# Two transformer blocks in float32: transitions of the second block as a pipeline of tiles

## The chip, the cores and the metric

The kernel runs on one core of a Trainium2 chip. The metric is the device time of one execution, in microseconds (us). Engines: PE multiplies matrices (PEld is its weight load), DVE and ACT work on vectors, POOL is the general engine, SP issues transfers.

## What is computed

A first block (latent and dilated attention, then a convolutional FFN) and a second, modulated block (attention, Fourier and Hyena mixers, then an FFN) run two layers each over 256 tokens of width 1024. The second block carries 256 context tokens through its layer 0; in layer 1 only keys and values are taken from them. Everything is float32. The parts that matter here are the second block's norms, shifts and gates:

```python
def rmsnorm_2(x, g):
    xf = x.astype(jnp.float32)
    y = xf * lax.rsqrt(jnp.mean(xf * xf, axis=-1, keepdims=True) + NORM_EPS)
    return (y * g.astype(jnp.float32)).astype(x.dtype)
...
        hx = rmsnorm_2(x, g_pre_mix[i]) * (1.0 + sc1) + sh1
        hc = rmsnorm_2(ctx, g_pre_mix[i]) * (1.0 + csc1) + csh1
        px = hx @ w_in[i]
...
        x = x + ga1 * rmsnorm_2(mix_x, g_post_mix[i])
...
        fx = rmsnorm_2(x, g_pre_ffn[i]) * (1.0 + sc2) + sh2
        yx = conv_ffn_2(fx, w_up[i], w_ffn_conv[i], b_ffn_conv[i], w_down[i])
        x = x + ga2 * rmsnorm_2(yx, g_post_ffn[i])
```

`sh`, `sc` and `ga` are slices of silu(c) @ w_mod + b_mod, one set for x and one for the context.

## The kernel before

**Matmuls.** A float32 product is made of three matmuls on high and low halves (`mm3`, L579, all recorded at L556). Features lie transposed in `hH`, `hL` (recorded as `hHL`). Weights come from HBM through `ring`, four slots of 1 MB, issued by SP in a fixed order (L1015). A piece of up to 1024 columns is copied to its high half by ACT (L1761, `wH`) and its low half subtracted by DVE (L1186, `wL`), by `splits_to` on both; three pieces rotate (`PIECES`), and `piece_used` gives one back. `piece_order` (L657) gives the last three pieces of a projection bank by bank. PSUM's eight banks are in two sets of four, `psv` read by DVE and `pss` read by ACT, opened in turn by `open_`, which waits for the bank's last reader.

**Order.** The program of each engine is written by hand. Each engine runs its instructions in that order, and semaphores join them (`V_full`, `S_free`, `root_ready` and so on), so an instruction that waits holds up all behind it on its engine.

**Stages.** First block, twice: features, `in` projections, latents (squares of the latent rows on ACT, small steps on DVE), lifts, rotary and dilated heads, attention, `out`, features, `up` with a convolution, `down` (22 pieces). Its own transitions already work by halves: add a half from PSUM to x (L1233, L1239), square the halves, `normalise1` with the gain as a broadcast row (L1249), transposes on PE (L606), high half by ACT and low half by DVE from PSUM (L1259). The next stage starts row by row (`have_rows`).

Second block, twice: modulation (`modulation_row` multiplies silu(c) by a chunk of w_mod, `modulation_col` turns it into columns `modc`; chunks `start`, `pairs`, `ffn`, `end` stand at different places), features, `hy`, q, k, v, Fourier, attention, `out`, features, `up`, `down`. Its transitions: ACT's `branch` copies odd tiles from PSUM to `mixo` and squares whole rows (`sumsq`, L1785 to L1788), DVE copies the even ones; `post` on DVE scales `mixo` by the inverse root and the gate row `gg` (L1594) and adds to x (L1596). Then `sumsq` of x, and `to_features`: four small steps of `inverse` (L1167 to L1173), a scaling by the row's inverse root (L1204), transposes, a scaling by gain column and shift column from PSUM (DVE L1216, ACT L1758) into `raw_h`, the high half by ACT and the low half by DVE (L1224). `have_features` lets the next stage begin when every tile is split. `modulation_ready` holds ACT's squares until the modulation columns exist. `keep_clock` issues matmuls without use, which fill PE's waits. POOL casts the FFN's products (L1038), and at the end stores x (L1054).

## Time and profile before

| | us |
|---|---|
| median of 3 runs | 1771.72 |
| lowest, highest | 1769.87, 1773.66 |
| profiled execution, its own time | 1769.04 |
| its span | 1767.3 |
| PE busy | 1639.4 (93%) |
| DVE busy | 1124.4 (64%) |
| ACT busy | 848.6 (48%) |
| POOL busy | 262.0 (15%) |

The span is the stretch from the first to the last recorded instruction; the execution's own time lies 1.7 us above it. The shares are averages over stages, so they say which engine bounds most of the time and not what a wait costs. The page's slices put PE's granted clock at nine tenths of full speed or more almost everywhere, with short dips.

### The profile page before, as it was taken

Reading aid. Unit: us, or ns where it says so; the run is one execution under the profiler, and the core shown is the slowest. Engines: PE = TensorE matmul, PEld = TensorE weight load, DVE = VectorE, ACT = ScalarE, POOL = GpSimd, SP = SyncE. Lnnn points to the kernel's source line nnn. Section 1 sums busy time; section 2 is a strip of 40 time slices with the busy share of each in tenths; the row PEclk is TensorE's granted clock in tenths of the full one; section 3 lists DMA queues with packets and bytes.
Section 4 is the critical chain, followed back from the end, with each engine's and each line's share of the span. In section 5 each row is a group of like instructions: output and inputs, shape, how many; then the busy total and the mean of one; then the engine's idle time right before and its main releaser. Section 6 shows DMA issues by size and latency. Waiting matters only on the chain. (4 is left out here: it accounts for less than half of the span.)

```text
span 1767.3 us, 22843 instructions
## 1 busy us (share of the span) xinstructions
PE 1639.4 (93%) x8628; PEld 1317.5 (75%) x8628; DVE 1124.4 (64%) x1875; ACT 848.6 (48%) x1518; POOL 262.0 (15%) x322
## 2 busy tenths in 40 slices
PE   7989999999999999899899899999999797989996
PEld 7667887886677887678467588888787595668875
DVE  5686898465868995553673744444333756579964
ACT  5554776355556664431353533333212534566742
POOL 2000113600021117000000001111630000001171
PEclk9999999999999999999999899999999799989998
DMA  7465765554578555523273533333222342246651
GB/s 261 151 209 172 202 189 180 193 167 166 198 225 246 145 170 169 161 78 96 94 237 111 155 96 96 96 96 96 96 95 96 102 138 66 72 124 187 184 185 48
DMA packets 266495, 258.32 MB, mean 146 GB/s; under 512 B 8821, under 2 KB 208729, under 8 KB 266130
## 3 DMA queue, kind: packets, MB, share of 16 engines
q1 hardware_dynamic: 262706, 245.36, 45.7%
q0 software_dynamic: 3536, 11.42, 1.8%
q8 instruction: 70, 1.15, 0.3%
q14 instruction: 39, 0.32, 0.1%
q10 hardware_dynamic: 144, 0.07, 0.0%
HBM read 255.72 MB, written 1.10 MB: 145 GB/s over the span
## 5 line engine op out<-in xcount | busy, mean ns | idle before, releaser
L556 PE MATMUL psv<-hHL,wH 128*128 128x512 f32 (+1 forms) x1952 | 644.2, 392 | 25.0 <-issue 21.1
L1186 DVE TENSOR_TENSOR wL<-ring,wH 128x1024 fp32r<-128x1024 f32 (+2 forms) x364 | 450.5, 1243 | 269.8 <-ACT wH L1761 266.7
L1761 ACT ACTIVATE wH<-ring 128x1024 fp32r<-128x1024 f32 (+2 forms) x364 | 376.1, 1040 | 302.1 <-PE psv L556 295.6
L556 PE MATMUL psv<-hHL,wL 128*128 128x256 f32 (+1 forms) x1504 | 468.5, 311 | 0.0
L556 PEld LDWEIGHTS psv<-hHL,wH 128*128 128x128 f32 x1952 | 368.2, 191 | 108.6 <-issue 23.3
L556 PE MATMUL psv<-wH,hHL 128*128 128x512 f32 (+2 forms) x936 | 319.2, 390 | 30.4 <-DVE wL L1186 17.6
L556 PEld LDWEIGHTS psv<-hHL,wL 128*128 128x128 f32 x1504 | 287.3, 191 | 15.9
L556 PE MATMUL pss<-wH,hHL 128*128 128x512 f32 (+3 forms) x808 | 274.4, 385 | 0.0
L556 PEld LDWEIGHTS psv<-wH,hHL 128*128 128x128 f32 x936 | 175.7, 189 | 74.4 <-DVE wL L1186 24.9
L556 PE MATMUL psv<-wL,hHL 128*128 128x512 f32 (+2 forms) x468 | 180.1, 385 | 0.0
L556 PEld LDWEIGHTS pss<-wH,hHL 128*128 128x128 f32 x808 | 152.5, 190 | 29.4
L1028 POOL TENSOR_TENSOR W<-scr 128x256 f32<-128x256 f32 (+1 forms) x88 | 81.7, 929 | 568.9 <-ACT scr L1918 568.9
L556 PE MATMUL pss<-wL,hHL 128*128 128x512 f32 (+3 forms) x404 | 155.2, 384 | 0.0
L1313 DVE SCALAR_TENSOR_TENSOR scr<-psv,colp,scr 128x510 f32<-128x510 f32 x44 | 33.0, 749 | 125.7 <-ACT scr L1910 125.7
L1761 ACT ACTIVATE scr<-psv 128x256 f32<-128x256 f32 x132 | 50.6, 384 | 126.7 <-PE psv L556 126.7
L1910 ACT ACTIVATE scr<-psv,colp 128x512 f32<-128x512 f32 x44 | 34.4, 781 | 155.0 <-PE psv L556 155.0
L556 PEld LDWEIGHTS psv<-wL,hHL 128*128 128x128 f32 x468 | 88.3, 189 | 16.1 <-issue 0.2
L1040 POOL TENSOR_TENSOR hHL<-W,hHL 128x256 fp32r<-128x256 f32 (+1 forms) x88 | 95.3, 1082 | 7.0
L556 PEld LDWEIGHTS pss<-wL,hHL 128*128 128x128 f32 x404 | 76.8, 190 | 14.6
L1314 DVE SCALAR_TENSOR_TENSOR scr<-scr,colp 128x255 f32<-128x255 f32 x132 | 79.7, 603 | 4.7
L1882 ACT ACTIVATE scr<-scr,colp 128x256 f32<-128x256 f32 x132 | 78.2, 592 | 2.3 <-DVE scr L1412 2.3
L1313 DVE SCALAR_TENSOR_TENSOR scr<-scr,colp 128x255 f32<-128x255 f32 x132 | 69.5, 526 | 4.3
(239 smaller groups left out, 1702.3 us busy)
## 6 DMA issues: line engine op xcount, KB each, us to landing
ring<-in_w_up SPq DMA_DIRECT2D x176, 512.0 KB, 5.2
ring<-in_w_mod SPq DMA_DIRECT2D x96, 512.0 KB, 4.8
ring<-in_w_down SPq DMA_DIRECT2D x88, 512.0 KB, 4.3
ring<-in_w_in SPq DMA_DIRECT2D x52, 512.0 KB, 4.6
ring<-in_w_out SPq DMA_DIRECT2D x32, 512.0 KB, 4.7
ring<-in_w_in SPq DMA_DIRECT2D x8, 384.0 KB, 6.0
ring<-in_w_in SPq DMA_DIRECT2D x8, 288.0 KB, 6.9
ring<-in_w_ukv SPq DMA_DIRECT2D x4, 512.0 KB, 4.2
```

Of the source, the lines that this page charges most:

```text
L556: return pe.matmul(o, a, b, start=start, stop=stop, skip_group_check=True)
L1028: gp.tensor_tensor(act[:, j, 0:ntok], cbuf(2 * j)[:, 0:ntok], cbuf(2 * j + 1)[:, 0:ntok], ALU.mult).then_inc(ffn_act, mark("ffn_act", ph, j))
L1040: gp.tensor_tensor(lo, a, hi.bitcast(F32), ALU.subtract).then_inc(act_split, mark("act_split", ph, j))
L1186: v.tensor_tensor(lo, raw, hi.bitcast(F32), ALU.subtract).then_inc(piece_split, told("piece_split", p))
L1313: return v.scalar_tensor_tensor(cv[:, :, 1:SEQ], bv_[:, :, 0:SEQ - 1], w0, cv[:, :, 1:SEQ], ALU.mult, ALU.add)
L1314: return v.scalar_tensor_tensor(cv[:, :, 0:SEQ - 1], bv_[:, :, 1:SEQ], w2, cv[:, :, 0:SEQ - 1], ALU.mult, ALU.add)
L1761: return ac.activation(o, i, ACT.Copy)
L1882: ac.activation(cbuf(n)[:, 0:SEQ], cbuf(n)[:, SEQ:2 * SEQ], ACT.Identity, scale=col(wname, l * 132 + 44 + u), bias=col(bname, l * 44 + u)) ...
L1910: ac.activation(cbuf(2 * j + g)[:, 0:ntok], b[:, 0:ntok], ACT.Identity, scale=col(wname, l * 132 + 44 + u), bias=col(bname, l * 44 + u)).t ...
```

## The change

In the second block, norm gains become rows: the columns (1 + scale) x gain are transposed by PE (`mix_rows`, `gates`), stored to DRAM and loaded back by POOL as `gain_rows`, broadcast to all partitions, for the mixer of the first layer in the middle of block 1's last FFN, for that of the second in the middle of layer 0's FFN. The normalise is one operation with the gain row (`normalise2`). The shift is added by PE: a matmul of `shift_rows` (its high and low halves) with `pick`, a selection matrix, into the bank of the transposes. The high and low halves are read from PSUM (`high_features2`, `low_features2`), and `raw_h` is gone; `xn4` holds four tiles of normalised rows. The post-norm works by halves: ACT squares each half in PSUM (`post_half`), DVE multiplies it by the gate row from PSUM (`gate_half`), and one operation scales and adds to x (`residual`). `transition` puts tiles behind one another on DVE and on ACT. The next stage begins at the last tile's first rows. The modulation at a layer's end moves into that transition. The context tiles of layer 0 are normalised and transposed inside block 1's last `down` (`CONTEXT_AT`).

In all four `down` projections the last piece's turn comes after two banks (`late`). In block 1 the small steps are three (`inverse1`), the dilated heads' transposes and copies come before the last input projection, the squares of the latents are taken together, and the first two pieces of `out` are split inside the attention's tail and no longer before it. x is stored from SP (tile 0, half of tile 1) and ACT (the other half), no longer from POOL.

```diff
-        raw_h = w_at(T0 + 4096, 2, KD, P)
+        gain_rows = w_at(T0 + 4096, 2, D)
+        xn4 = w_at(T0 + 6144, 4, D)
...
+        CONTEXT_AT = {11: 2, 13: 3}
...
+            def feature_tile(ph, t, x, banks=None):
+                pe.wait_ge(rows_normalised, at("rows_normalised", ph, t))
+                for (kind, b), k0 in zip(banks or feature_banks(ph, t), (0, 4)):
+                    for k in range(4):
+                        settle(pe.matmul(b[:, k * P:(k + 1) * P], x[:, (k0 + k) * P:(k0 + k + 1) * P], ident[:, :], start=k == 0, stop=False,
+                                         is_transpose=True, skip_group_check=True))
+                    c = 16 + 8 * (t // 2) + k0
+                    mm(b.rearrange("p (k n) -> p k n", k=4), shift_rows[:, :], pick[:, c:c + 4].unsqueeze(2).to_broadcast([64, 4, P]),
+                       False, True).then_inc(FULL[kind], mark(kind + "_full", ph, "hT", t))
...
+                turns = [(i, q) for i in range(len(banks)) for q in range(m, n)]
+                if late:
+                    turns = [(i, q) for i in (0, 1) for q in range(m, n - 1)] + [(0, n - 1), (1, n - 1)] + turns[2 * (n - m):]
...
-                for (t, h, kind, b), j, w in piece_order(banks, NJ, True):
+                for (t, h, kind, b), j, w in piece_order(banks, NJ, True, True):
                     if (t, h) == (0, 0):
+                        if ahead and j in CONTEXT_AT:
+                            c = CONTEXT_AT[j]
+                            feature_tile(context, c, xn[:, c % 2, :], ahead[c])
...
+            sp.wait_ge(residual_updated, at("residual_updated", ("b2", L - 1), "ffn", 0, 1))
+            sp.dma_start(out[0, 0:P, :], xs[:, 0, :]).then_inc(out_stored, mark("out_stored", "all", by=16))
+            sp.wait_ge(residual_updated, at("residual_updated", ("b2", L - 1), "ffn", 1, 1))
+            sp.dma_start(out[0, P:2 * P, 512:D], xs[:, 1, 512:D]).then_inc(out_stored, mark("out_stored", "all", by=16))
+            sp.wait_ge(out_stored, at("out_stored", "all"))
+            sp.wait_ge(half_stored, 16)
...
+            def load_mix_rows(l):
+                gp.wait_ge(gate_stored, at("gate_stored", l, "mix"))
+                load(gain_rows[:, :, :], rows_of(mix_dram[l], 2), "gain_rows_in", l, "mix")
...
-                        v.tensor_scalar(xn[:, t % 2, :], xs[:, t, :], rr[:, t:t + 1], None, ALU.mult).then_inc(rows_normalised, told("rows_normalised", ph, t))
...
+            def gate_half(ph, what, stage_, t, h):
+                kind, key, n = "VS"[t % 2], (ph, what, h, t) if what == "out" else (ph, what, t, h), slice(h * 512, (h + 1) * 512)
+                v.wait_ge(gate_in, at("gate_in", ph, stage_))
+                v.wait_ge(sum_of_squares, at("sum_of_squares", ph, "post", stage_, t, *(() if h else ("half",))))
+                v.tensor_tensor(mixo[:, t, n], bank(kind, *key), gg[:, t // 2, n], ALU.mult).then_inc(FREE[kind], told(kind + "_free", *key))
...
+            def residual(ph, what, stage_, t):
+                kind, key = "VS"[t % 2], (ph, what, 1, t) if what == "out" else (ph, what, t, 1)
+                v.wait_ge(root_ready, at("root_ready", ph, "post", stage_, t))
+                inverse1(4 + t)
+                v.wait_ge(FREE[kind], at(kind + "_free", *key))
+                v.scalar_tensor_tensor(xs[:, t, :], mixo[:, t, :], rr[:, 4 + t:5 + t], xs[:, t, :], ALU.mult, ALU.add).then_inc(residual_updated, told("residual_updated", ph, stage_, t))
...
+            def normalise2(ph, t, x):
+                v.wait_ge(root_ready, at("root_ready", ph, t))
+                inverse1(t)
+                v.wait_ge(gain_rows_in, at("gain_rows_in", ph[1], ph[2]))
+                v.scalar_tensor_tensor(x, xs[:, t, :], rr[:, t:t + 1], gain_rows[:, t // 2, :], ALU.mult, ALU.mult).then_inc(rows_normalised, told("rows_normalised", ph, t))
...
+            def transition(ph, what, stage_, nph, first, cs):
+                nt = 4 if ph[1] == 0 else 2
+                for t in range(nt):
+                    if t >= 2:
+                        normalise2(nph, t - 2, xn4[:, t - 2, :])
+                    for h in range(1 if what == "out" else 0, 2):
+                        gate_half(ph, what, stage_, t, h)
+                    residual(ph, what, stage_, t)
+                normalise2(nph, nt - 2, xn4[:, nt - 2, :])
+                splits_to(first, 0)
+                normalise2(nph, nt - 1, xn4[:, nt - 1, :])
+                for c in cs[:-1]:
+                    modulation_col(1, c)
+                for t in range(nt):
+                    low_features2(nph, t, cs)
+                    if t == 1:
+                        for c in cs[-1:]:
+                            modulation_col(1, c)
...
-                splits_to(first_piece[ph, "out", 0], 1)
...
+                attention(ph, units1, 0, MOD1[l]["pairs"], mla_columns, (first_piece[ph, "out", 0], (8, 9)))
...
+                if l == L - 1:
+                    nph = ("b2", 0, "mix")
+                    splits_to(first_piece[ph, "down"] + 8, 0)
+                    v.wait_ge(block2_in, at("block2_in", "all"))
+                    v.wait_ge(ffn_act, at("ffn_act", ph, NJ - 1))
+                    for t in (2, 3):
+                        normalise2(nph, t, xn[:, t % 2, :])
+                        splits_to(first_piece[ph, "down"] + 2 * t + 5, 0)
+                    for t in (2, 3):
+                        splits_to(first_piece[ph, "down"] + 2 * t + 8, 0)
+                        low_features2(nph, t)
...
+            def post_half(ph, what, stage_, t, h):
+                kind, bk, key = "VS"[t % 2], (ph, what, h, t) if what == "out" else (ph, what, t, h), (ph, "post", stage_, t)
+                ac.wait_ge(FULL[kind], at(kind + "_full", *bk))
+                if h:
+                    other_half(bank(kind, *bk), 4 + t, t, *key)
+                else:
+                    half_sum(bank(kind, *bk), t, *key)
...
+            def transition(ph, what, stage_, nph, first, cs):
+                nt = 4 if ph[1] == 0 else 2
+                last_key = (ph, what, 1, nt - 1) if what == "out" else (ph, what, nt - 1, 1)
+                def norm(t):
+                    ac.wait_ge(residual_updated, at("residual_updated", ph, stage_, t))
+                    sumsq(xs[:, t, :], D, t, nph, t)
+                def row(i):
+                    if i >= len(cs):
+                        return
+                    ac.wait_ge(S_free, at("S_free", *last_key))
+                    ac.wait_ge(S_full, at("S_full", "modrow", 1, cs[i]))
+                    if i:
+                        ac.wait_ge(V_full, at("V_full", "modcol", 1, cs[i - 1]))
+                    copy(mrow[:, :], bank("S", "modrow", 1, cs[i])).then_inc(S_free, mark("S_free", "modrow", 1, cs[i]))
+                for t in range(nt):
+                    for h in range(1 if what == "out" else 0, 2):
+                        post_half(ph, what, stage_, t, h)
+                    if nt == 4 and t in (1, 2):
+                        norm(t - 1)
+                if nt == 2:
+                    norm(0)
+                    splits_to(first, 0)
+                    norm(1)
+                else:
+                    norm(2)
+                    row(0)
+                    splits_to(first, 0)
+                    norm(3)
+                    row(1)
+                for t in range(nt):
+                    high_features2(nph, t)
...
+                attention(ph, units1, mla_columns, (first_piece[ph, "out", 0], (8,)))
...
+            ac.wait_ge(residual_updated, at("residual_updated", ("b2", L - 1), "ffn", 1, 0))
+            ac.dma_start(out[0, P:2 * P, 0:512], xs[:, 1, 0:512]).then_inc(half_stored, 16)
```

On DVE, in the second block's layer 0, from its output projection to its FFN (T2 below). `xs` is x (four tiles of 128 tokens, the last two of context), `W` here the mixed rows, gains or normalised rows, `rr` the inverse root. Before, from the update of tile 2 on:

```order
L1596 TENSOR_TENSOR xs<-xs,W 128x1024
L1167 RECIPROCAL rr<-root 128x1
L1169 TENSOR_TENSOR nwt<-rr 128x1
L1171 SCALAR_TENSOR_TENSOR nwt<-nwt,ss 128x1
L1173 SCALAR_TENSOR_TENSOR rr<-nwt,rr 128x1
L1594 SCALAR_TENSOR_TENSOR W<-W,rr 128x1024
L1596 TENSOR_TENSOR xs<-xs,W 128x1024
L1167 RECIPROCAL rr<-root 128x1
L1169 TENSOR_TENSOR nwt<-rr 128x1
L1171 SCALAR_TENSOR_TENSOR nwt<-nwt,ss 128x1
L1173 SCALAR_TENSOR_TENSOR rr<-nwt,rr 128x1
L1204 TENSOR_SCALAR scr<-xs,rr 128x1024
```

Now, from the update of tile 1 on:

```order
L1304 SCALAR_TENSOR_TENSOR xs<-W,rr,xs 128x1024
L1346 RECIPROCAL rr<-root 128x1
L1348 SCALAR_TENSOR_TENSOR nwt<-rr,ss 128x1
L1350 SCALAR_TENSOR_TENSOR rr<-nwt,rr 128x1
L1311 SCALAR_TENSOR_TENSOR W<-xs,rr,W 128x1024
L1296 TENSOR_TENSOR W<-psv,W 128x512
L1346 RECIPROCAL rr<-root 128x1
L1348 SCALAR_TENSOR_TENSOR nwt<-rr,ss 128x1
L1350 SCALAR_TENSOR_TENSOR rr<-nwt,rr 128x1
L1304 SCALAR_TENSOR_TENSOR xs<-W,rr,xs 128x1024
L1346 RECIPROCAL rr<-root 128x1
L1348 SCALAR_TENSOR_TENSOR nwt<-rr,ss 128x1
```

The first normalise (L1204 before, L1311 now) stood behind all four updates; it now stands behind tile 1's, and the gates (L1296) read PSUM.

On DVE a little further on, the end of that same hand-over. Before, the last tiles' features and then the weight halves of the FFN's first pieces (L1186):

```order
L1204 TENSOR_SCALAR scr<-xs,rr 128x1024
L1341 TENSOR_TENSOR modc<-psv,colp 128x2x4
L1216 TENSOR_SCALAR W<-psv,modg,modc 128x128 x4
L1224 TENSOR_TENSOR hHL<-W,hHL 128x8x128
L1216 TENSOR_SCALAR W<-psv,modg,modc 128x128 x4
L1224 TENSOR_TENSOR hHL<-W,hHL 128x8x128 x2
L1186 TENSOR_TENSOR wL<-ring,wH 128x1024 x3
L1313 SCALAR_TENSOR_TENSOR scr<-psv,colp,scr 128x2x255
```

Now, from the third tile's normalise on:

```order
L1311 SCALAR_TENSOR_TENSOR W<-xs,rr,W 128x1024
L1252 TENSOR_TENSOR wL<-ring,wH 128x1024
L1346 RECIPROCAL rr<-root 128x1
L1348 SCALAR_TENSOR_TENSOR nwt<-rr,ss 128x1
L1350 SCALAR_TENSOR_TENSOR rr<-nwt,rr 128x1
L1311 SCALAR_TENSOR_TENSOR W<-xs,rr,W 128x1024
L1468 TENSOR_TENSOR modc<-psv,colp 128x2x4
L1320 TENSOR_TENSOR hHL<-psv,hHL 128x4x128
L1320 TENSOR_TENSOR hHL<-pss,hHL 128x4x128
L1320 TENSOR_TENSOR hHL<-psv,hHL 128x4x128
L1320 TENSOR_TENSOR hHL<-pss,hHL 128x4x128
```

One weight half (L1252) now stands ahead of the last tile's normalise, and the low halves (L1320) are taken straight from PSUM.

On ACT, in the first block's layer 0, around the attention's end; `wH<-ring` is the high half of a weight piece, `scr,den<-pss,mx` the exponentials. Before:

```order
L1761 ACTIVATE scr<-pss 128x512 x2
L1864 ACTIVATE scr,den<-pss,mx 128x256 x4
L1761 ACTIVATE scr<-pss 128x512 x2
L1864 ACTIVATE scr,den<-pss,mx 128x256 x4
L1761 ACTIVATE scr<-pss 128x512 x4
L1810 ACT_TABLE_LOAD
L1810 ACTIVATE root<-eps_col 128x1
L1761 ACTIVATE wH<-ring 128x1024 x6
```

Now:

```order
L2049 ACTIVATE scr,den<-pss,mx 128x256 x4
L1898 ACTIVATE scr<-pss 128x512 x2
L2049 ACTIVATE scr,den<-pss,mx 128x256 x4
L1898 ACTIVATE scr<-pss 128x512 x2
L1898 ACTIVATE wH<-ring 128x1024
L1898 ACTIVATE scr<-pss 128x512 x2
L2007 ACT_TABLE_LOAD
L2007 ACTIVATE root<-eps_col 128x1
L1898 ACTIVATE wH<-ring 128x1024 x7
```

One weight copy now stands among the attention's last copies; before, the output projection's first pieces were split ahead of the attention.

## Rows read from the trace of the kernel before

**Rows 1.** The page, part 1: busy time of each engine, share of the span, instructions.
```profile
PE 1639.4 (93%) x8628; PEld 1317.5 (75%) x8628; DVE 1124.4 (64%) x1875; ACT 848.6 (48%) x1518; POOL 262.0 (15%) x322
```

**Rows 2.** Table by stretch: length, PE, PEld, DVE, ACT, POOL busy, PE's granted clock, DMA, GB/s.
```profile
733.15:755.43 22.28, 14.11 (x75) 10.31 (x73) 18.29 (x50) 18.70 (x39) 0.00 (x0) 0.80 0.31 95
755.43:760.50 5.07, 5.07 (x12) 4.01 (x13) 2.16 (x2) 0.34 (x1) 0.00 (x0) 0.51 0.57 180
982.55:1009.24 26.69, 17.93 (x110) 11.50 (x109) 24.09 (x58) 21.36 (x46) 0.53 (x1) 0.88 0.71 197
...
1377.04:1410.33 33.29, 20.54 (x105) 14.86 (x103) 24.86 (x63) 22.06 (x49) 0.00 (x0) 0.77 0.47 127
...
1543.93:1560.70 16.77, 8.78 (x40) 7.03 (x39) 14.27 (x30) 12.86 (x26) 0.53 (x1) 0.85 0.10 32
...
1752.23:1767.30 15.07, 0.39 (x2) 0.00 (x0) 5.26 (x8) 2.23 (x5) 1.13 (x2) 0.66 0.18 70
165.68:172.69 7.01, 6.34 (x54) 4.41 (x53) 6.52 (x12) 4.75 (x11) 0.54 (x1) 1.00 0.52 146
```

**Rows 3.** Timeline of PE: start, us, engine, line, operation, [idle before <-releaser].
```profile
755.43 1.19 PE L556 MATMUL psv<-hHL,wH 128*128 128x512 f32 x2 [5.58 <-issue]
...
1385.33 1.86 PE L556 MATMUL psv<-fold,mrow 128*128 128x2 f32 x8 [4.33 <-DVE mrow L1335]
```

**Rows 4.** Timeline: five rows of T1, and two of block 1's own transition.
```profile
736.51 0.16 DVE L1167 RECIPROCAL rr<-root 128x1 f32<-128x1 f32 x1 [1.80 <-ACT ss L1788]
...
737.29 0.75 DVE L1204 TENSOR_SCALAR scr<-xs,rr 128x1024 f32<-128x1024 f32 x1
...
738.10 0.66 PE L606 MATMUL pss<-ident,scr 128*128 128x128 f32 x4 [1.21 <-DVE scr L1204]
...
740.04 1.36 DVE L1216 TENSOR_SCALAR W<-psv,modg,modc 128x128 f32<-128x128 f32 x4
...
752.96 1.23 DVE L1224 TENSOR_TENSOR hHL<-W,hHL 128x1024 fp32r<-128x1024 f32 x1 [0.18 <-ACT hHL L1761]
...
169.16 1.28 DVE L1249 SCALAR_TENSOR_TENSOR scr<-xs,rr,W 128x1024 f32<-128x1024 f32 x1
...
170.37 0.68 DVE L1259 TENSOR_TENSOR hHL<-psv,hHL 128x512 fp32r<-128x512 f32 x1
```

**Rows 5.** Timeline of SP in T2, and the page's part 6: KB each, median us to landing.
```profile
984.81 14.48 SPq L1015 DMA_DIRECT2D ring<-in_w_up  x8
...
ring<-in_w_up SPq DMA_DIRECT2D x176, 512.0 KB, 5.2
```

**Rows 6.** Timeline of POOL in block 1's last FFN, and part 6 for a row broadcast.
```profile
684.58 1.40 POOL L1038 CAST hHL<-W 128x256 fp32r<-128x256 f32 x1
...
W<-gate_scratch POOLq DMA_DIRECT2D x2, 1024.0 KB, 6.0
```

**Rows 7.** Groups of PE by line with their idle time, and two waits in the timeline.
```profile
L556 PE MATMUL psv<-wH,hHL 128*128 128x512 f32 (+2 forms) x936 | 319.2, 390 | 30.4 <-DVE wL L1186 17.6 <-POOL hHL L1040 4.8 <-DVE scr L1314 3.6
...
L556 PE MATMUL psv<-W 64*128 64x256 f32 (+5 forms) x114 | 23.9, 417 | 9.4 <-DVE W L1543 8.6 <-DVE modc L1341 0.8
...
353.92 0.50 PE L556 MATMUL psv<-wH,hHL 128*128 128x512 f32 x1 [1.28 <-DVE wL L1186]
...
41.36 0.50 PE L556 MATMUL psv<-wH,hHL 128*128 128x512 f32 x1 [2.61 <-DVE wL L1186]
```

**Rows 8.** Timeline at the end of block 1's first attention, ACT and PE.
```profile
141.62 1.28 ACT L1810 ACT_TABLE_LOAD   x1
...
143.73 0.50 PE L556 MATMUL psv<-wH,hHL 128*128 128x512 f32 x1 [0.98 <-DVE hHL L1193]
144.07 0.40 PE L556 MATMUL psv<-wL,hHL 128*128 128x512 f32 x1
144.30 0.40 PE L556 MATMUL psv<-wH,hHL 128*128 128x512 f32 x1
```

**Rows 9.** Timeline of POOL at the end.
```profile
1758.65 1.13 POOL L1054 DMA_DIRECT2D out<-xs  x2 [27.78 <-DVE xs L1596]
```

484 lines of the change are left out of this document (264 added, 220 removed).

## The prediction

> **What bounds the kernel now.** I read the busy shares first: the matmul engine PE works 1639.4 of 1767.3 us, 93% of the span, DVE 64%, ACT 48% [rows 1]. So only the places where PE idles, or is kept busy with filler, can give time back. Next the timeline of PE, and the table by stretch, over each place where one stage hands to the next. Five stretches stand out [rows 2]: from the last matmul of block 1 to the first of block 2 (22.28 us, call it T1), block 2 layer 0 from its output projection to its FFN (T2, 26.69), its FFN to layer 1's mix (T3, 33.29), layer 1's output projection to its FFN (T4, 16.77), and the end (T5, 15.07). PE's busy time inside them (14 of 22 us in T1) is mostly filler, transposes and modulation. The same table has block 1's own transition, which already works by halves from PSUM with the norm gain as a row: 7.01 us, at a granted clock of 1.00. After T1 the granted clock stands at 0.51 for 5.07 us [rows 2], the 1.2 GHz level, PE having waited 5.58 us just before [rows 3]. The rest of PE's idle time is in short waits on the weight halves and on the attention's inputs [rows 7, 8].
>
> **T1.** Today the first features come by a chain: squares of all of x, four small DVE steps (736.51 to 737.29, 0.78 us), the scaling 0.75, transposes, gain and shift per column 1.36, the low halves from SBUF 1.23 for each of four tiles [rows 4]. The new chain is that of block 1: three small steps and a row-form normalise of 1.28, transposes, low halves from PSUM at 0.68 per 512 columns [rows 4]. I take block 1's 7.01 us, and add 0.9 for four 512-column shift matmuls on PE and the wait for both latent tiles: 7.9, so -14.4. The context tiles' transposes move into block 1's last down projection, where PE is the bound: four transposes take 0.66 [rows 4], so 16 take 2.6 at most, less where they cover a wait; with four shift matmuls and none of it hidden I charge +2.7. At 7 us of hand-over block 1 keeps its clock, so half of the 5.07 slow us goes too: -2.5. T1 in all -14.2 (bounds -9 to -17: the clock stays slow; the transposes hide).
>
> One new wait is on the way there. The context tiles' normalise on DVE waits for the gain rows, which POOL loads after its eighth FFN cast and subtraction, some 2.4 us behind the cast at 684.58; a 1024 KB broadcast takes 6.0 us to land [rows 6], so they are there at 693, and the normalise is through at 694.3. Queued behind it on DVE is a weight half that PE needs at 696.0. It is hidden by 0.5 to 1.5 us; a load of 9 us would cost 2 to 3, once.
>
> **T2.** Before, four residual updates, each a scaling and an addition of 1024 columns (1.28 and 1.23 by their like in [rows 4]), come before the first normalise. After, tile 0 is normalised as soon as tile 1's residual is in. Let E be the last matmul. The four output banks end 4.1 us apart (three pieces of six matmuls, one each 0.23 us [rows 8]). On DVE a residual or a normalise costs 1.28 plus three small steps of 0.2, 1.88 us; a gate of half a tile from PSUM about 0.7, like the low half's 0.68. Walking the queue: tile 0 normalised before E, tile 2's residual E+0.2, tile 1 normalised +2.1, tile 3's gate and residual +4.7, tile 2 normalised +6.6. Then, ahead of tile 3's normalise, DVE splits the first weight piece. Its DMA is issued after the modulation chunk frees the slot, at E+2 (984.81), and lands 5.2 later [rows 5], ACT copies it by E+8.2, DVE is through at 9.4, tile 3 normalised at 11.8 (ACT's part of the small steps included), and eight low halves at 0.61 to 0.68 end at 16.8. The FFN takes all four tiles as one moving operand, so it starts at E+17: -9.7. Without the wait for the weight it would be 14, -12.7; if gates wait for their squares too, 20, -7.
>
> **T3.** The same queue, plus two modulation columns that must come before the features. Before, they stood behind the whole post-norm chain (PE waits 4.33 us for them at 1385.33 [rows 3]) and the features began only after them. After, they follow the last normalise, and modulation's last rows are made a layer ahead. The same walk gives 17.5 of 33.29: -15.8 (bounds -12 to -19).
>
> **T4.** Two tiles. Tile 1's last gate at E+1.8, residual 3.9, squares and normalise 8.6, transposes, high and low halves of the second tile to 11.0 of 16.8: -5.5 (bounds -4 to -7). I give T2 to T4 no clock back: they stay over 10 us with filler inside.
>
> **T5.** Before, whole-row squares follow the last copy, then scaling and addition, and only then POOL issues both stores at 1758.65, 1.13 us of issuing [rows 9], some 6 us behind the last matmul (1752.2 [rows 2]). After, one square of 512 is left behind the last matmul, a gate of 0.7, three small steps, and two 512-column updates of 0.7; tile 0 is stored 3 to 4 us earlier and tile 1 in two quarter-megabyte stores from two queues. x is ready 3.6 instead of 5.9 us after the last matmul (-2.3). From the issue to the span's end is now 8.65 us (1767.3 less 1758.65); without POOL's 1.13 of serial issuing, and with half the bytes left behind the last update, I take 6.85: -1.8. Together -4.1 (bounds -1 to -6). The Trainium skill, "DMA: Bandwidth & Descriptors" (Issuing engine by pattern, and Latency), says that DMAs issued from SyncE or ScalarE have their first byte after about 0.6 us against 1 us from GpSimd, and that most of a DMA's fixed part of some 2 us is the write receipt, which halving the bytes doesn't touch. By that page alone the store would give 0.4 plus the smaller transfer; no row here shows the two issuers at the same store.
>
> **Short waits.** In each of four down projections PE waits 1.28 us for DVE's half of the last piece (the first at 353.92 [rows 7]; the others are alike). Taking that piece's turn after two banks gives DVE 2 us more: 4 x 1.28 = -5.1. The latents' squares are now taken in a batch with four small operations after them, and a third piece is split ahead of them. PE's wait of 2.61 there in layer 0, with about half as much in layer 1, goes but for 0.4: -3.5; all waits of this form for DVE's weight halves are 17.6 us [rows 7], so this and the tails make half of them. Attention start: the dilated transposes and copies go ahead of the last input bands, and DVE no longer splits the output's first pieces there. PE's waits there, 8.6 us in the two layers [rows 7], go: with 0.6 of a shorter queue before it -4.7 in layer 0, and -6.0 in layer 1, where a wait for a weight half before the bands shrinks too. The two splits come back inside the attention's tail. There DVE's second split follows ACT's copy, which stands behind the 1.28 us table load at 141.62; it pushes the last cast of the attention's output by 2.5 us and the projection that starts at 143.73 [rows 8] to 146.3: +2.6, and +1.5 in layer 1, where modulation covers more. Net -2.1 and -4.5. Small: -0.5 for shorter inverses in block 1, +1.5 for the row transposes, shift splits and their places in queues.
>
> **Sum.** -14.2 -9.7 -15.8 -5.5 -4.1 -5.1 -3.5 -6.6 +1.0 = -63.5. Against the profiled run's own 1769.04 that is 1705.5; the median of the runs is 2.7 above that run, so 1708.2.
>
> **A rule against the change.** The old normalise, one tensor times a per-row scalar from SBUF, takes 0.75 us for 1024 columns, the new one with a gain tensor 1.28 [rows 4]. The Trainium skill, "VectorE: DVE Perf Modes" (Mode 2x_2P, and Rules for kernel authors), says the first form gets twice the rate in float32 by using both read ports, a form with two tensors doesn't, and anything from PSUM doesn't either; it advises a copy to SBUF where many operations follow. The trace agrees (753 against 1284 ns). For 14 tiles the price is 14 x 0.53 = 7.4 us of DVE, of which the part on the path is in my walks. If that part outweighed the rest, T1 to T4 would lose 7.4 of their 45 us and the time be 1716. But each tile sheds 1.36 + 1.23 - 2 x 0.68 = 1.2 us of DVE, and ACT's 1.5 of scaling, so I give it no case of its own.
>
> **Rivals.** (a) The first weight piece isn't late, or its split doesn't hold up the last normalise: T2 and T3 at 14 us, 6 less: 1702. For it: block 1's first weights are there in a 7 us hand-over. Against: the slot is freed by the same modulation chunk. 0.2. (b) New waits eat a third of T1 to T4: gates must wait for ACT's squares of the same bank and hold banks that the transposes want, and the clock stays at 1.2 GHz after T1. T1 12, T2 21, T3 23, T4 13.5: +16, and +2.5 of clock; 1727. For it: ACT and DVE are in one chain per tile, and the walk has each hand-over at its shortest. 0.27. (c) The attention's splits cost more than the waits they replace (the change doesn't do there what it says): instead of -6.6, +4, other things as forecast: 1719. 0.1. (d) Slower: the clock. T1 shows a half-rate stretch after a wait. If the new order, with less filler in front of each stage, left PE at 1.2 GHz for long stretches, each us of full-speed work there costs one more; it decides once 64 us of such work run at half clock beyond what does so now, and 68 give 1776. The stretch seen after T1 is 5.07 us, so it has 0.03.
>
> **How the numbers follow.** Forecast 0.4 (1703 to 1715), (a) 0.2, (b) 0.27, (c) 0.1, (d) 0.03. The predicted time is the likeliest, 1708. The range leaves out (d), the lower edge of (a) and the worst of (b): 1695 to 1731. About 0.2% (3.5 us) is what a measurement of this kernel can tell from no change; all cases but (d) are faster by more: 0.96 faster, 0.01 the same, 0.03 slower.
>
> **What would show it.** In the profile after: PE from last to first matmul 8, 17, 17.5 and 11 us at T1 to T4; a granted clock of 1.00 behind T1; DVE's first weight split at T2 waiting for ACT with the last normalise behind it; no 1.28 us waits late in the down projections; attention starting within 1 us of PE's last work, its projection some 2 us later than its last cast would allow; two half stores and no POOL at the end. Wrong would be: a T2 over 20 us with the gates waiting for ACT, a DVE wait for the gain rows around 693 with PE idle behind it, or a clock below 0.9 over a whole stage.

## The result, and the profile after

The changed kernel takes 1717.4 us (median; runs from 1712.1 to 1719.4) against 1770.8 before: a ratio of 0.970, interval 0.968 to 0.972. The profiled run took 1718.0 and spans 1716.2. So 51.1 us of span went, where 63.5 were forecast. (Of the kernels under Experiments, one execution took 4138 us and another 9223, for no reason that the record shows; neither enters a number.)

The page of the changed kernel, its first line, the busy times that answer to [rows 1], and the group of PE that answers to the first of [rows 7]:

```profile
span 1716.2 us, 22859 instructions
...
PE 1642.1 (96%) x8638; PEld 1314.7 (77%) x8638; DVE 1108.8 (65%) x1816; ACT 833.4 (49%) x1520; POOL 265.6 (15%) x329
...
L564 PE MATMUL psv<-wH,hHL 128*128 128x512 f32 (+2 forms) x936 | 321.5, 393 | 22.6 <-DVE wL L1252 7.5
```

PE works as long as before (1642.1 us against 1639.4); what went is idle time. In this group the waits for a weight half fell from 17.6 to 7.5 us.

The table by stretch of the changed kernel: T1, the stretch behind it, T2, T3, T4, T5, then block 1's first output projection. Columns are those of [rows 2]:

```profile
730.93:740.28 9.35, 8.77 (x55) 5.19 (x53) 7.81 (x13) 7.21 (x14) 0.00 (x0) 1.00 0.64 196
740.28:745.35 5.07, 5.07 (x24) 4.18 (x23) 1.51 (x2) 0.06 (x1) 0.00 (x0) 1.00 0.76 262
965.20:987.42 22.22, 19.77 (x106) 12.65 (x105) 13.43 (x27) 10.64 (x24) 1.59 (x3) 0.85 0.89 240
1352.25:1375.35 23.10, 20.44 (x106) 12.76 (x105) 14.58 (x30) 10.94 (x26) 0.00 (x0) 0.85 0.68 182
1505.91:1521.70 15.79, 13.50 (x51) 9.57 (x49) 11.57 (x20) 9.43 (x19) 0.53 (x1) 0.78 0.08 33
1709.67:1716.20 6.53, 0.39 (x2) 0.00 (x0) 3.53 (x8) 1.17 (x4) 0.00 (x0) 0.71 0.43 163
140.40:164.70 24.30, 24.30 (x95) 19.63 (x96) 10.18 (x13) 9.25 (x15) 0.00 (x0) 0.89 0.59 173
```

And the same output projection in the kernel before:

```profile
143.73:165.68 21.95, 21.95 (x96) 17.88 (x96) 10.37 (x14) 9.47 (x15) 0.00 (x0) 1.00 0.50 144
```

Read against [rows 2]: the clock behind T1 is 1.00 where it was 0.51, twice as many matmuls stand in the same 5.07 us, and T5 is less than half. But T2 and T3 are 5.2 and 5.6 us longer than forecast, at a clock of 0.85, and T4 is hardly shorter than its old 16.77. Block 1's output projection, which the change hardly touches, has become 2.35 us longer at 0.89.

The whole, stretch by stretch (profiled runs, us):

| place | forecast | measured |
|---|---|---|
| T1, clock behind it, context tiles | -14.2 | -10.0 (-12.9 -2.2 +5.1) |
| T2 | -9.7 | -4.5 |
| T3 | -15.8 | -10.2 |
| T4 | -5.5 | -1.0 |
| clock behind T2, T3, T4 | 0 | -1.9 -2.7 -2.2 |
| T5 | -4.1 | -8.5 |
| four ends of down projections | -5.1 | -5.3 |
| block 1: to the start of both output projections | -10.1 | -10.0 |
| block 1: the output projections themselves | 0 | +3.9 |
| block 1: first up stage (pace of its matmuls) | 0 | +2.1 |
| small | +1.0 | -0.8 |
| sum | -63.5 | -51.1 |

Each row rests on one execution of either kernel, and a hand-over can differ between executions of the same order. The kernel before has T1 at 22.3 and 21.2 us in its two traces and T2 at 26.7 and 25.4. T1 has the same instructions in eleven traces of changed kernels: it takes 9.3 us at full clock in eight, and 11.0 to 11.5 in three, where the clock falls in it though PE's waits are the same. One of the three, by stretch (the kernel with stores from SP alone):

```profile
730.31:741.83 11.52, 10.95 (x54) 6.92 (x53) 9.31 (x14) 7.25 (x14) 0.00 (x0) 0.81 0.62 188
```

T2 and T3 as the change has them take 22.1 to 23.3 and 21.6 to 23.1 us in six traces. So a row is good to 1 or 2 us, and the experiments below are judged by their medians first.

### The profile page after: what moved, and what is told of

It is laid out like the page before. It is cut to its first block, busy times and chain, and to the rows that moved or that the text cites. A ratio compares the mean times of both kernels' runs of the same rounds, so it can differ in the third digit from the quotient of the medians.

```text
span 1716.2 us, 22859 instructions
## 1 busy us (share of the span) xinstructions
PE 1642.1 (96%) x8638; PEld 1314.7 (77%) x8638; DVE 1108.8 (65%) x1816; ACT 833.4 (49%) x1520; POOL 265.6 (15%) x329
## 4 chain that ended last, share of the span: by engine, by line
PE 81%; DVE 10%; ACT 4%; DMA 2%; issue 2%; SPq 1%; DVEq 0%; ACTq 0%
PE psv L564 60%; PE pss L564 18%; DVE wL L1252 2%; PE pss L614 2%; DMA ring<-in_w_up 1%; ACT scr L2049 1%; DVE scr L1441 1%; SPq L1030 1%; ACT wH L1898 1%; PE psv L614 1%; DVE scr L1440 1%; SPq L1049 1%; ACT scr L1898 1%; DVE W L1673 0%; ACT L2007 0%
## 5 line engine op out<-in xcount | busy, mean ns | idle before, releaser
L1252 DVE TENSOR_TENSOR wL<-ring,wH 128x1024 fp32r<-128x1024 f32 (+2 forms) x364 | 452.7, 1248 | 260.6 <-ACT wH L1898 257.5
L564 PEld LDWEIGHTS psv<-hHL,wH 128*128 128x128 f32 x1952 | 363.4, 188 | 87.0 <-DVE wL L1252 6.8
L564 PEld LDWEIGHTS psv<-hHL,wL 128*128 128x128 f32 x1504 | 283.6, 189 | 15.8
L1441 DVE SCALAR_TENSOR_TENSOR scr<-scr,colp 128x255 f32<-128x255 f32 x132 | 80.0, 606 | 4.7
L1078 POOL CAST hHL<-W 128x256 fp32r<-128x256 f32 (+1 forms) x88 | 63.0, 716 | 67.5 <-PE psv L564 66.2
```

Source lines behind the costliest of these rows:

```text
L564: return pe.matmul(o, a, b, start=start, stop=stop, skip_group_check=True)
L1078: gp.tensor_copy(hi, a).then_inc(act_high, mark("act_high", ph, j))
L1252: v.tensor_tensor(lo, raw, hi.bitcast(F32), ALU.subtract).then_inc(piece_split, told("piece_split", p))
L1441: return v.scalar_tensor_tensor(cv[:, :, 0:SEQ - 1], bv_[:, :, 1:SEQ], w2, cv[:, :, 0:SEQ - 1], ALU.mult, ALU.add)
```

## What T2 looks like now

Timeline of the changed kernel in T2, all engines, the rows that decide. Columns: start, us, engine, line, operation, [idle before <-releaser]:

```profile
965.52 3.64 PE L564 MATMUL pss<-ring,csil 128*32 128x512 f32 x32
...
969.92 1.28 DVE L1311 SCALAR_TENSOR_TENSOR W<-xs,rr,W 128x1024 f32<-128x1024 f32 x1
...
973.35 1.06 ACT L1898 ACTIVATE wH<-ring 128x1024 fp32r<-128x1024 f32 x1 [4.48 <-DMA ring<-in_w_up]
...
974.43 1.23 DVE L1252 TENSOR_TENSOR wL<-ring,wH 128x1024 fp32r<-128x1024 f32 x1 [3.23 <-ACT wH L1898]
...
976.49 1.87 PE L564 MATMUL psv<-fold,mrow 128*128 128x2 f32 x8 [2.45 <-ACT mrow L1898]
...
976.63 1.28 DVE L1311 SCALAR_TENSOR_TENSOR W<-xs,rr,W 128x1024 f32<-128x1024 f32 x1
...
978.22 4.66 PE L564 MATMUL psv<-colp,ident 128*128 128x256 f32 x12
...
982.71 0.60 PE L628 MATMUL psv<-ident,W 128*128 128x128 f32 x4
983.76 0.60 ACT L1898 ACTIVATE hHL<-psv 128x512 fp32r<-128x512 f32 x1 [5.38 <-PE psv L564]
```

ACT waits 4.48 us for the first piece of `in_w_up`, and DVE 3.23 for ACT: the forecast's late weight piece. The last tile is normalised at 977.9 (976.63 + 1.28), which is E+12.7 with E = 965.20: the forecast said E+11.8. So the walk over DVE was near. But T2 doesn't wait for that normalise: what it left out are ACT's and PE's queues. Behind the first two tiles' transposes stands a modulation column, whose row copy (`mrow`) stands on ACT behind the weight copy and the last tile's squares; PE waits 2.45 us for it. Behind that stand six fillers, 12 records that take 4.66 us. Tile 2 has been normalised since 971.2, and its transposes begin at 982.71. Followed back from its end, the chain of T2 goes over PE, the row copy, the squares and the weight copy on ACT to the DMA, and not over DVE.

## Experiments

All ratios are to the kernel before. The first four ask which of the two, fillers or the late piece, lengthens T2 and T3.

**No filler in T2 and T3**

```diff
-                        (0, 6, 0, 2) if l else (0, 4))
+                        (0, 0, 0, 0) if l else (0, 4))
...
-                        (0, 5) if last else (0, 6, 0, 2))
+                        (0, 5) if last else (0, 0, 0, 0))
```

> The changed kernel without the filler matmuls between and behind the tiles' transposes at T2 and T3 (8 of 256 columns each: 6 behind the second tile, 2 behind the fourth). Theory A (the filler is on the path): in the changed kernel PE runs the 6 fillers at 1.2 GHz, 978.2 to 982.7 at T2, while tile 2 and 3 have been normalised since 971.2 and 977.9. Without them tile 2's transposes start at 978.4: T2 22.2 -> 17.8, T3 23.1 -> 18.5, in all 8 to 9 us faster if the clock behind stays at 1.00. Theory B (the filler pays for itself): without it PE's clock is at 1.2 GHz behind T2 and T3 for about 5 us as in the kernel before, 2 to 2.7 us each, and the net gain is 4 us or less. A rival C: ACT and DVE, not PE, set the end of T2 (low halves queued behind the weight half): T2 and T3 shorter by under 1 us.

1713.4 us, 0.9674 [0.9649, 0.9699]: 4 us less than the changed kernel, with overlapping intervals. T2 and the stretch behind it:

```profile
967.07:986.97 19.90, 17.62 (x91) 9.95 (x89) 13.38 (x26) 9.96 (x22) 1.59 (x3) 0.75 0.90 243
986.97:992.00 5.03, 5.03 (x16) 4.00 (x16) 3.05 (x3) 2.49 (x3) 0.00 (x0) 0.65 0.55 141
```

T2 is 2.3 and T3 3.2 us shorter, but the clock is at 0.75 in T2 and still at 0.65 behind it: 35% of that stretch is lost. The fillers paid for part of themselves. Taking them away alone isn't the cure, since PE still waits for the piece.

**The same, and the weight piece split behind the last normalise**

```diff
                 normalise2(nph, nt - 2, xn4[:, nt - 2, :])
-                splits_to(first, 0)
                 normalise2(nph, nt - 1, xn4[:, nt - 1, :])
+                splits_to(first, 0)
```

(and likewise `splits_to(first, 0)` behind the last `norm` on ACT, in addition to the edit above)

> As the run without filler at T2 and T3, and in every transition of the second block the first weight piece is split after the last tile's normalise on ACT and DVE, not ahead of it. If the wait for that piece's DMA (ACT waits 4.48 us at T2, 3.88 at T3) holds up the last normalise, as the prediction's walk had it (2.8 us each), T2 is 15 and T3 15.5, and T4 1.2 shorter (13.1 -> 11.9): 5 to 7 us below the run without filler. Rival: the modulation column behind the last normalise, or the weight half now late itself, takes its place: under 2 us.

1702.2 us, 0.9629 [0.9595, 0.9663]: 11.2 us less than the run above, where 5 to 7 were expected (the intervals just overlap). Its profiled run was its slowest, 1713.2 (the others 1700.5 to 1703.6), and shows T3 at 15.05 and T4 at 11.71 us, but T2 at 23.03. The timeline of T2 in it says why:

```profile
973.25 16.00 SPq L1049 DMA_DIRECT2D ring<-in_w_up  x8
...
984.51 1.06 ACT L1898 ACTIVATE wH<-ring 128x1024 fp32r<-128x1024 f32 x1 [7.18 <-DMA ring<-in_w_up]
...
987.00 1.09 PE L628 MATMUL psv<-ident,W 128*128 128x128 f32 x4 [6.18 <-issue]
```

The piece comes by two DMAs of 512 KB, and ACT waits for both. In this execution it had them 11.3 us after the first was issued (973.25 to 984.51); in the changed kernel it was 5.9 (967.45 to 973.35). ACT's queue has the weight copy ahead of the features, so all waited. Behind the last normalise is a better place than between the last two, yet still ahead of work that doesn't need the piece.

**The weight piece split amid the features**

```diff
                     low_features2(nph, t, cs)
+                    if t == nt // 2 - 1:
+                        splits_to(first, 0)
...
                     high_features2(nph, t)
+                    if t == nt // 2 - 1:
+                        splits_to(first, 0)
```

(`splits_to(first, 0)` taken from its old places; fillers out of T2 and T3 as above)

> No filler at T2 and T3, and the next stage's first weight piece is split behind the features of the middle tile (the second of four, the first of two) on ACT and DVE. Where the piece is split before the features, everything behind it on ACT waits for its DMA: in the profiled run with the piece behind the last normalise that DMA took 11.3 us at T2 (issued 973.25, landed 984.5), ACT waited 7.18 us, and T2 took 23.0, where the other runs with that kernel were 10 to 13 us faster than the profiled one. Theory: behind the features the late piece holds back nothing but the first matmul, T2 is 16 to 18 in any run, T3 15, T4 12, the median 1701 as for the piece behind the last normalise, but with the runs closer together. Rival: the spread comes from the clock at T1 and T2 and stays.

1696.2 us, 0.9579 [0.9561, 0.9596]. Its T2, T3 and T4 in the table by stretch:

```profile
963.62:977.85 14.23, 13.72 (x90) 7.57 (x89) 13.21 (x26) 10.77 (x23) 1.59 (x3) 1.00 0.79 225
...
1342.62:1357.27 14.65, 13.79 (x91) 7.57 (x89) 14.08 (x29) 10.97 (x26) 0.00 (x0) 1.00 0.88 220
1488.86:1500.57 11.71, 10.34 (x50) 7.66 (x49) 9.61 (x19) 8.88 (x19) 0.53 (x1) 1.00 0.13 45
```

14.2, 14.7 and 11.7 us at full clock: close to what the forecast gave as "without the wait for the weight" (14) and to its 11.0. But in T2 it isn't DVE that bounds, as the walk had it. The last normalise, the start of that tile's transposes, and the first matmul behind T2:

```profile
970.18 1.28 DVE L1311 SCALAR_TENSOR_TENSOR W<-xs,rr,W 128x1024 f32<-128x1024 f32 x1
...
975.28 0.66 PE L628 MATMUL psv<-ident,W 128*128 128x128 f32 x4
...
977.85 0.70 PE L564 MATMUL psv<-hHL,wH 128*128 128x512 f32 x2 [0.51 <-DVE hHL L1320]
```

The last tile is normalised at 971.46, E+7.8 with this run's E = 963.62, and waits 3.8 us for PE, which is at work without a listed wait from 967.51 to 977.34: modulation, its two columns, and the transposes and shifts of four tiles. PE is busy 13.7 of the 14.2 us, DVE 13.2. In T3 the two are as full, and there the chain runs over DVE.

**The same with the fillers back**

> The weight piece amid the features, as in the run of that name, but with the 8 filler matmuls at T2 and T3 kept. It tells the filler's part from the weight wait's. If the filler alone holds PE at T2 and T3: 6 fillers of 0.12 us at full clock are 0.7 us, at half clock 1.4, and T2 and T3 are 15 to 16 us with the clock at 1.00, since PE waits for little; median 1697 to 1700. If filler and late weight piece each cost by themselves, T2 stays at 18 or more and the median at 1704 or more.

This is the kernel just above, with T2's and T3's fillers as the change has them. 1702.3 us, 0.9621 [0.9603, 0.9639]:

```profile
962.48:979.55 17.07, 17.07 (x107) 10.53 (x105) 13.35 (x27) 10.97 (x24) 1.59 (x3) 1.00 0.87 235
1344.15:1361.52 17.37, 17.13 (x106) 10.52 (x105) 14.41 (x30) 11.05 (x25) 0.00 (x0) 1.00 0.88 240
```

So the fillers cost 2.84 and 2.72 us at full clock, most of the 3.5 us that they take on PE in T2 (2.68 and 0.78), and guard nothing once the piece is out of the way: the clock is 1.00 with and without them. My expectation had them far cheaper, since I took a filler for one short matmul. Each is two records of 256 columns, `colp,ident`; the four fillers in T1 are eight records that take 1.97 us. Together these runs split T2: 14.2 for the queues of PE and DVE, 2.8 for fillers, 5.2 for the late piece with the half clock that it brings; T3 is 14.7, 2.7 and 5.7. (The 5.2 and 5.7 carry the spread of the changed kernel's T2 and T3.)

**Both first pieces of the output projection split ahead of the attention, as before the change**

```diff
-                attention(ph, units1, mla_columns, (first_piece[ph, "out", 0], (8, 9)))
+                attention(ph, units1, mla_columns)
...
                 v.tensor_copy(dvh[:, 0, :, :], ...)
+                splits_to(first_piece[ph, "out", 0], 1)
```

(and the like on ACT; the modulation chunk goes back between the weight loads)

> The changed kernel with one part undone: the first two pieces of block 1's output projection are split ahead of the attention as in the kernel before, and the chunk order is put back. Theory: the attention starts 2.4 us later (the two low halves), but the projection follows its last cast within 1 us, and its first 5 us are not at 1.2 GHz, which cost 2.4 us in layer 0 and about 1.6 in layer 1. Sum: +4.8 for the starts, -2.5 and -1.5 at the ends, -4 for the clock: 2 to 4 us faster than the changed kernel. Rival: the clock falls behind attention in any case: 0 to 1 us slower.

1717.0 us, 0.9698 [0.9682, 0.9713]: no gain where 2 to 4 us were expected. The wait ahead of the output projection is gone, and another has come at the attention's start. First the changed kernel, the second group of PE's matmuls in layer 0's attention and the first matmul behind it, then this one:

```profile
93.27 1.13 PE L564 MATMUL psv<-W 64*128 64x256 f32 x8
...
140.40 0.80 PE L564 MATMUL psv<-wH,hHL 128*128 128x512 f32 x1 [3.42 <-DVE hHL L1259]
```

```profile
95.50 1.13 PE L563 MATMUL psv<-W 64*128 64x256 f32 x8 [2.41 <-DVE mx L1403]
...
141.16 0.50 PE L563 MATMUL psv<-wH,hHL 128*128 128x512 f32 x1 [0.99 <-DVE hHL L1258]
```

The output projection starts 0.8 us later than in the changed kernel, though the wait ahead of it fell from 3.42 to 0.99 us: the two splits on DVE now delay `mx`, the row maxima that the attention needs first. The clock fell behind this attention too (0.60 from 141.16 to 144.00). By the start of layer 0's FFN both kernels are level (171.4 and 171.5). In layer 1 the clock held and the projection was 21.9 us long, 1.6 less, but it began 3.4 later (489.1 against 485.7). This profiled run still spans 1.6 us less than the changed kernel's, by shorter transitions in block 2 that the edit doesn't touch; the medians are the same.

**One of the two splits early** (run after the others, on top of the weight split amid the features)

```diff
-                attention(ph, units1, mla_columns, (first_piece[ph, "out", 0], (8, 9)))
+                attention(ph, units1, mla_columns, (first_piece[ph, "out", 0], (8,)))
```

(DVE takes its share of one piece among the attention's steps and that of the other behind the casts)

> The kernel with the weight piece amid the features and no filler at T2 and T3, and DVE splits one piece of block 1's output projection inside the attention's tail, not two. With two, DVE's second split waits 2.41 us for ACT's copy behind the table load, and the last cast of the attention's output stands behind it: PE waits 3.42 us. My prediction priced that at 2.6 us in layer 0 and 1.5 in layer 1. If so, the output projection starts 2.5 us earlier after the attention in layer 0 and 1 to 1.5 in layer 1, PE waits 1 us, and since the clock fell to 1.2 GHz in that wait, the projections keep 1.00 and are 21.95 us long as in the kernel before, not 23.5: together 5 to 7 us, median 1690. Rival: the projection's second piece is late instead, PE waits for it 1 to 2 us, and the clock falls all the same: under 2 us.

1690.8 us, 0.9549 [0.9522, 0.9576]: the fastest of all, 26.6 us below the changed kernel and 5.4 below the kernel it is built on, as expected (that kernel's interval and this one's just overlap). PE at the attention's end, and both output projections in the table by stretch:

```profile
138.17 0.50 PE L564 MATMUL psv<-wH,hHL 128*128 128x512 f32 x1 [0.99 <-DVE hHL L1259]
```

```profile
138.17:160.11 21.94, 21.94 (x96) 17.87 (x96) 11.52 (x14) 10.60 (x17) 0.00 (x0) 1.00 0.64 192
479.67:501.57 21.90, 21.90 (x96) 17.87 (x96) 11.57 (x15) 9.61 (x16) 0.00 (x0) 1.00 0.85 277
```

The wait fell from 3.42 to 0.99 us and the clock behind it is 1.00. It was ACT's copy and DVE's split ahead of the last cast that cost: in the run it is built on, the same projection took 23.48 us at 0.93. From its start to the output projection, the attention is 2.44 us shorter in layer 0 and 1.44 in layer 1.

**The filler moved from T1 to the attention's end**

```diff
-                        (0, 0, 0, 0) if l else (0, 4))
+                        (0, 0, 0, 0) if l else (0, 0))
...
                 attention(ph, units1, 0, MOD1[l]["pairs"], mla_transposes)
+                keep_clock("S", 14)
```

(on top of the split amid the features)

> The kernel with the weight piece amid the features and no filler at T2 and T3, with two more edits. The 4 fillers at T1 go: PE runs them until 740.1 while the features are there since 739.2, so T1 is 9.3 -> 8.4 if they are on the path. 14 fillers come behind block 1's attention, where PE waits 3.4 us for the last cast and the clock then stands at 1.2 GHz for 4 to 5 us of the output projection: if they keep the clock, each of block 1's output projections is 2 us shorter, the start of it later by 0 to 0.5 us. Median 1692 to 1693 against 1696. Rival: the fillers run at half clock themselves and delay the projection by 1 us or more: no gain there.

1699.9 us, 0.9605 [0.9583, 0.9628]: 3.6 slower than the kernel it is built on, with overlapping intervals. T1 and what follows, then the output projection behind the fillers:

```profile
735.39:743.34 7.95, 7.39 (x46) 3.99 (x45) 6.54 (x11) 5.82 (x13) 0.00 (x0) 0.97 0.61 174
743.34:747.00 3.66, 3.66 (x11) 2.95 (x12) 2.76 (x4) 1.44 (x2) 0.00 (x0) 0.60 0.72 218
142.75:164.73 21.98, 21.98 (x97) 17.93 (x96) 9.14 (x12) 9.29 (x15) 0.00 (x0) 1.00 0.54 164
```

T1 is 1.38 us shorter, 7.95: the 7.9 of the forecast, which had no filler in it. But the clock behind it is 0.60 for 3.66 us, and the projections that follow it take 60.00 us up to their first long break, against 58.75. So the fillers in T1 give back about what they cost, and no more. At the attention's end 14 fillers do keep the clock (21.98 us, clock 1.00) but take 6.31 us where 3.42 were idle; the projection starts 2.7 us later than in the kernel it is built on and gains 1.5. In layer 1 the attention ends 4.4 us later for the same 1.5. Filler buys the clock there at more than it is worth.

**The context tiles four places later in the down projection**

```diff
-CONTEXT_AT = {11: 2, 13: 3}
+CONTEXT_AT = {15: 2, 17: 3}
```

(the splits around them moved by the same four)

> The context tiles' normalise and transposes inside block 1's last down projection come four pieces later, when POOL has nearly done with its casts and the gain rows have long landed. In the changed kernel DVE's 1024-column subtraction takes 1.76 us there instead of 1.23 and a small step 0.73 instead of 0.22, beside POOL's work, and PE waits 0.70; the whole projection is 5.1 us longer than the 1.28 saved explains, where I had 2.7. If POOL's neighbourhood is the cause, the 0.70 us wait goes and the projection is 0.7 to 1.5 us shorter. If it is the transposes and shift matmuls themselves (1.94 us for each tile on PE), it stays within 0.7 us.

1717.4 us, 0.9704 [0.9687, 0.9722]: no change. The down projection took 66.4 us against 66.9, and 63.0 before the change: the wait of 0.71 us in it fell to 0.16, and the rest stayed. So neither the gain rows nor the place make most of the cost. The timeline of the changed kernel at one of the tiles:

```profile
693.95 0.50 PE L564 MATMUL psv<-wH,hHL 128*128 128x512 f32 x1 [0.71 <-DVE wL L1252]
...
696.83 0.60 PE L628 MATMUL psv<-ident,scr 128*128 128x128 f32 x4
...
697.36 0.48 PE L564 MATMUL psv<-pick,shift_rows 64*128 64x512 f32 x1
...
697.77 0.44 PE L628 MATMUL pss<-ident,scr 128*128 128x128 f32 x2
```

A group of four transposes takes 0.53 us and a shift matmul 0.41 to the next instruction (697.36 to 697.77), so a tile 1.9 and both 3.9 of PE's own time. The rest of the 5.1 is one wait of 0.71 and about 0.5 in smaller gaps.

**Without the late turn of the down projections' last piece**

```diff
-            piece_order(banks, NJ, True, True)
+            piece_order(banks, NJ, True, False)
```

> The changed kernel without the later turn of the last piece in the four down projections. Theory: PE waits 1.28 us for DVE's half in each of the four again, +5.1 us. Rival: in the changed kernel the pieces come earlier or later there, so that some of the waits are not back.

1720.2 us in its one run, span 1718.4 against 1716.2. The wait of [rows 7] is back, and the group's waits for DVE's `wL` go from 7.5 to 12.6 us, 5.1 = 4 x 1.28:

```profile
353.87 0.50 PE L564 MATMUL psv<-wH,hHL 128*128 128x512 f32 x1 [1.28 <-DVE wL L1252]
...
L564 PE MATMUL psv<-wH,hHL 128*128 128x512 f32 (+2 forms) x936 | 320.5, 391 | 27.9 <-DVE wL L1252 12.6 <-DVE hHL L1259 6.6 <-POOL hHL L1080 4.7
```

The four down projections are 1.3 to 1.4 us longer each. The span as a whole grew by only 2.2, mainly because T4 was 12.7 us long in this execution where it is 15.8 in the changed kernel's.

**The stores from POOL, and from SP alone**

```diff
+            gp.wait_ge(residual_updated, at("residual_updated", ("b2", L - 1), "ffn", 1, 1))
+            for t in range(NT):
+                load(out[0, t * P:(t + 1) * P, :], xs[:, t, :], "out_stored", "all")
```

(the stores of SP and ACT taken out)

> The changed kernel with x stored by POOL as two whole tiles after the last update, as before. The end took 6.5 us from the last matmul in the changed kernel against 15.07 before; my prediction had 11. If the issuing engine and the size make the difference, the span from the last update's end to the span's end goes from 2.7 back to about 8.7 us (+6); if it was the earlier readiness of tile 0, only +1 to +2.

```diff
-            sp.dma_start(out[0, P:2 * P, 512:D], xs[:, 1, 512:D])...
+            sp.dma_start(out[0, P:2 * P, :], xs[:, 1, :])...
-            ac.dma_start(out[0, P:2 * P, 0:512], xs[:, 1, 0:512])...
```

> The changed kernel with both tiles of x stored whole by SP, none by ACT. The end took 6.5 us from the last matmul in the changed kernel, 13.4 with POOL's two stores. If the issuing engine makes the difference, it is 7 to 8 (a 512 KB store lands 1 to 2 us later than 256 KB); if the split in quarters makes it, 11 or more.

1728.0 and 1717.3 us in one run each. From the last matmul to the end of the span it is 6.5 us in the changed kernel, 6.9 with SP's one store of the last tile, and 13.4 with POOL's two stores. The last update and the issue in the three kernels, changed, SP, POOL:

```profile
1712.13 1.42 DVE L1744 SCALAR_TENSOR_TENSOR xs<-W,rr,xs 128x512 f32<-128x512 f32 x2
...
1713.58 0.34 SPq L1053 DMA_DIRECT2D out<-xs  x1
```

```profile
1711.00 1.41 DVE L1743 SCALAR_TENSOR_TENSOR xs<-W,rr,xs 128x512 f32<-128x512 f32 x2
1712.44 0.34 SPq L1053 DMA_DIRECT2D out<-xs  x1
```

```profile
1714.55 1.41 DVE L1742 SCALAR_TENSOR_TENSOR xs<-W,rr,xs 128x512 f32<-128x512 f32 x2
1716.26 1.12 POOL L1091 DMA_DIRECT2D out<-xs  x2 [24.18 <-DVE xs L1742]
...
out<-xs POOLq DMA_DIRECT2D x2, 512.0 KB, 3.4
```

From the issue to the end: 2.6, 3.1 and 9.2 us (1716.2 - 1713.58, 1715.5 - 1712.44, 1725.5 - 1716.26). POOL's stores landed after a median of 3.4 us, so some 4 to 5 us of the 9.2 lie behind the landing and 1.1 in the issue. Splitting the tile in two quarters is worth 0.4. POOL's kernel also has both tiles, 1 MB, behind the last update, where SP's has one; what that costs by itself isn't measured, but it can only lie ahead of the landing. So at least 4 us come from the engine that issues the stores and waits for them; the edit moves both, and no run tells them apart.

**The kernel before, once more**

> The kernel before, once more, for two readings. First, in block 1's first up projection its pairs of a 512 and a 256 column matmul came every 0.3467 us, in all nine changed kernels so far every 0.3533, at a granted clock of 1.00 in both; in block 2's last one both values occur in either. If the 0.3467 belongs to the kernel before, it comes again (2.3 us over the stage are then part of the change); if it varies from run to run, it may be 0.3533. Second, T1 to T4: 22.3, 26.7, 33.3 and 16.8 us, each with 3.8 to 5.5 us at 1.2 GHz behind it, within 1 us.

1771.5 us, span 1769.7. T1 to T4 are 21.2, 25.4, 33.3 and 16.8 us in it, with half clock behind each; T1 and T2 miss the expected 1 us by a little, so that much is chance between executions. So the clock behind T2 to T4 was low in the kernel before in both of its traces. It also shows the pace of block 1's first up stage again. There, a weight being split in a high and a low part, a matmul of 512 columns and one of 256 follow each other; such a pair starts every 0.3467 us, over the stage, in both traces of the kernel before and every 0.3533 in all traces of changed kernels. 22 x 2 x 8 = 352 pairs make 2.3 us, the +2.1 of the table. The granted clock is 1.00 in both. In block 2's last up stage the pace is 0.3533 in both traces of before, and either value in the changed ones. What sets it stays open.

## Why the forecast came out as it did

The time, 1717.4, is 9 us above the 1708.2 forecast and inside the range. The sum is nearer than its parts: within T2 to T4 15.3 us less came than forecast, 4.2 less at T1 and 6.1 less in block 1's attentions, output projections and first up stage; the clock behind T2 to T4 gave 6.8 that weren't counted, T5 4.4 more, and the small terms 1.8 more. That 13 us of unforeseen gain stood against 26 of loss is luck, and without it the time would lie near the range's upper end.

- **T1.** 9.35 us, forecast 7.9. The step that failed is the list of added work: it has no term for the four fillers that stay there. They take 1.4 us by the run that moved them, and without them T1 is 7.95. The four shift matmuls, which the 0.9 was meant for, take 0.41 us each to the next instruction, 0.7 more than that; the rest of the stretch was as much shorter. "Half of the 5.07 slow us goes too": 2.2 came, against 2.5, and with the fillers gone it would not have come.
- **Context tiles.** +5.1, forecast +2.7 with "none of it hidden". Mis-sized: four shift matmuls (1.6 us) were covered by 0.1 of it, so PE's own time is 3.9 (16 transposes take 2.1 to 2.3), and 1.2 came in a new wait and gaps. The wait for the gain rows, which the forecast let be hidden by 0.5 to 1.5 us, is indeed nowhere on PE.
- **T2 and T3.** 22.2 and 23.1, forecast 17 and 17.5. Right was that the weight piece comes late, that its split holds up the last normalise, and that without it the time is some 14. The failed step is that the walk followed DVE only. The piece costs by way of ACT, where it holds up the row copy of the modulation column; PE's queue had that column and six fillers between the second and the third tile's transposes, and the clock is half for what stands behind the wait. The last normalise ends 4.8 us before the third tile's transposes begin, so it isn't what T2 waits for. That T2 without the piece comes to the 14 of the walk is partly luck: there the normalise ends at E+7.8, where the walk less its 2.8 us of waiting has E+9.0, and PE's own work fills the rest. Late piece and clock cost 5.2 and 5.7 us where 3 and 3.5 were charged, the fillers 2.8 and 2.7 where nothing was.
- **T4.** 15.8, forecast 11.0 (16.8 less 11.0 is 5.8, where the sum has 5.5). The walk is near at full clock: 11.7 in five of the kernels, its five fillers included, and 12.7 in two that leave the weight piece where the change puts it; five others that do, the changed kernel among them, have 15.5 to 15.8 at 0.78 to 0.81. So the piece costs about 1 us, and the half clock (0.78 over the stretch) some 3; "they stay over 10 us with filler inside" ruled out a gain behind them and no loss within.
- **"I give T2 to T4 no clock back."** Wrong by 6.8 us in the other direction. The kernel before ran its next stages at half clock for a while after each; the changed one doesn't. The same order has a low clock within the hand-over instead.
- **T5.** -8.5, forecast -4.1 with -6 as its end. x is ready 3.9 us after the last matmul's start (1713.55 less 1709.67), forecast 3.6: near (before the change it was 6.1 and not 5.9). The failed step is "I take 6.85" from the issue to the end, a guess within POOL's own numbers; it is 2.6. The Trainium skill, "DMA: Bandwidth & Descriptors" (Latency and other measured facts), puts the first byte of a DMA at about 0.6 us from SP or ACT and 1 us from POOL. The traces don't show first bytes; from issue to the span's end they show 6.2 us between POOL and SP at this place, of which the page's 0.4 is a small part, and the measurement decides.
- **Tails of the down projections.** -5.3, forecast -5.1; the run without the late turn gives 5.1 back.
- **Attention.** -10.0 to the start of the two output projections, forecast -4.3 and -5.8 (starts, latents and the splits inside), so -10.1. The start came 7.1 us earlier in layer 0 (97.22 to 90.14), forecast 6.9. The splits at the end cost as priced (2.6 and 1.5; 2.44 and 1.44 by the run with one early split). The failed step is that a wait was priced there at its length alone. The clock fell behind PE's waits of 3.42 us in layer 0 and 1.45 in layer 1, and the projections behind them took 2.35 and 1.6 us more:

```profile
485.72 0.50 PE L564 MATMUL psv<-wH,hHL 128*128 128x512 f32 x1 [1.45 <-DVE hHL L1259]
```

- **The longer normalise.** DVE takes 1.28 us for it in the changed kernel as well, against 0.75 for the old form in [rows 4]. The Trainium skill, "VectorE: DVE Perf Modes" (Mode 2x_2P), says that only a form with one tensor gets the double rate in float32, and the two durations agree. The price didn't outweigh the rest.

Of the rivals, (a) needed the late piece away from the last normalise; its 14 us came only with that edit. (b) came near the sizes of T2 and T3 (21 and 23) for another reason, and had the clock at the wrong place: low behind T1, where it was low within T2 to T4. T2's last gate (966.83) starts without a wait for ACT's squares. (c) did not come: the splits cost what was charged. (d) did not come: the mean clock of the profiled run rose from 0.973 to 0.981. Of the signs that the prediction named for being wrong, one came, a clock below 0.9 over the whole of T2, T3 and T4, and one came in half: T2 over 20 us, but not by its gates.

## What to carry to other kernels

Walk a hand-over on every engine's queue, the bound engine's own first: what is queued between two steps of the chain, a modulation column, filler or a weight copy, delays them as much as a slow operation does. On each in-order queue, put work that depends on a DMA behind as much as possible of the work that does not: without filler, the same split made 19.9 us of T2 in one place and 14.2 in another. And price a new wait of PE with the clock of what follows it.

## What the runs showed of the hardware

- Two final stores issued and awaited by POOL ended the span 9.2 us after their issue though they had landed after a median of 3.4. Where SP issued the last store and waited, it was 2.6 to 3.1 us.
- The clock fell behind a wait of 3.42 us at the attention's end (to the 1.2 GHz level, 0.50 from 140.40 to 145.00) in all nine traces with that wait, behind one of 1.45 to 1.50 in layer 1 in eight of nine, and held behind one of 0.99 in the fastest kernel and 0.98 in the kernel before. It isn't the last wait alone: with both splits ahead of the attention it fell as well (0.60), at waits of 0.80 and 0.99 that the fastest kernel has too. And in T1 it fell in three of eleven traces with the same instructions and waits. What decides between them stays open.
- The two 512 KB DMAs of a weight piece had landed 11.3 us after the first was issued in one execution, 5.9 us in another at the same place.
- A matmul of 64 rows and 512 columns for the shift takes 0.41 us to the next, a like one of 128 rows in a projection 0.23.
- Pairs of matmuls run at 0.3467 or 0.3533 us at the same granted clock; the cause stays open.
